# Mixture of experts on one core: down product one block later, weights in three buffers by expert

## The reference

```python
p_group = softmax(h @ w_rg + b_rg);  pg, grp = top_k(p_group, 1)
le_g = (h @ w_re + b_re)[group grp];  we, ei = top_k(softmax(le_g), 2)
gates = pg * we / sum(we)                      # two experts of each token
for e in range(16):
    a = silu(h @ w_eg[e]) * (h @ w_eu[e])      # 1024 -> 256, twice
    out = out + gates[:, e] * (a @ w_ed[e])    # 256 -> 1024
```

## Time and profile before

| | us |
|---|---|
| three runs | 1703.21, 1734.66, 1704.06 |
| median of them | 1704.06 |
| span of the profiled execution, first to last instruction | 1733.6 |
| time of the profiled execution | not listed by itself; of the three runs only the highest, 1734.66, is as long as its span |
| blocks 2 to 31 of the experts' stage | 1280 to 1669 of the span |

### The profile page before, as it was taken

How to read it: one execution, slowest core, us unless ns; L and a number is a source line. 1 busy time by engine, 2 the same in 40 slices (tenths; PEclk the granted TensorE clock), 3 DMA queues, 4 the chain that set the end, 5 groups by cost and what they waited for, 6 DMA issues and landing times.

```text
span 1733.6 us, 15660 instructions
## 1 busy us (share of the span) xinstructions
PE 1518.5 (88%) x5392; PEld 867.8 (50%) x5392; DVE 626.5 (36%) x1253; ACT 378.9 (22%) x788; POOL 135.1 (8%) x202
## 2 busy tenths in 40 slices
PE   7899999996099998999999999999589999999940
PEld 2575433432055473886777775455444444444420
DVE  2204339999813269611111232324401111111119
ACT  4114210030124210132233352111011111111114
POOL 0100100000000202101000000000021111111131
PEclk9899989998599869565555699999589999999975
DMA  9102652100030002406000000111198999999945
GB/s 348 43 1 97 192 184 76 49 1 0 0 73 1 3 25 70 125 2 157 0 1 0 1 1 25 68 66 41 47 355 329 336 335 331 332 343 323 341 166 188
DMA packets 78230, 219.98 MB, mean 127 GB/s; under 512 B 26205, under 2 KB 40733, under 8 KB 62791
## 3 DMA queue, kind: packets, MB, share of 16 engines
q1 hardware_dynamic: 61436, 163.70, 27.2%
q0 software_dynamic: 16736, 55.51, 8.8%
HBM read 191.07 MB, written 28.11 MB: 126 GB/s over the span
## 4 chain that ended last, share of the span: by engine, by line
PE 71%; DVE 13%; issue 11%; ACT 3%; DMA 1%; SPq 1%; DVEq 0%; POOL 0%; ACTq 0%; POOLq 0%
PE psum L1269 13%; PE psum L1208 7%; PE psum L878 7%; PE psum L1286 7%; PE psum L1132 7%; PE psum L1176 5%; DVE marks L1738 4%; PE psum L836 4%; PE psum L1162 4%; PE psum L901 2%; PE psum L1082 2%; PE psum L1144 1%; DVE mem L1669 1%; PE psum L1227 1%; PE psum L1278 1%
## 5 line engine op out<-in xcount | busy, mean ns | idle before, releaser
L878 PE MATMUL psum<-mem 128*128 128x512 f32 (+5 forms) x576 | 179.5, 471 | 61.2 <-ACT mem L1368 55.5
L1269 PE MATMUL psum<-mem 128*128 128x512 f32 x512 | 228.0, 599 | 1.1 <-ACT mem L1579 1.1
L901 PE MATMUL psum<-mem 128*128 128x512 f32 (+1 forms) x480 | 165.7, 511 | 0.0
L878 PEld LDWEIGHTS psum<-mem 128*128 128x128 f32 (+1 forms) x576 | 95.8, 186 | 137.4 <-issue 75.0
L1269 PEld LDWEIGHTS psum<-mem 128*128 128x128 f32 x512 | 98.3, 192 | 125.3 <-issue 123.8
L1949 DVE CUSTOM_DVE_ANT_0 mem<-psum,mem 128x1024 f32<-128x1024 f32 (+3 forms) x64 | 48.4, 758 | 242.1 <-PE psum L1132 242.1
L1286 PE MATMUL psum<-mem 128*128 128x512 f32 x256 | 118.4, 605 | 15.2 <-ACT mem L1589 15.2
L1208 PE MATMUL psum<-mem 128*128 128x512 f32 (+1 forms) x288 | 127.3, 602 | 0.7 <-issue 0.7
L901 PEld LDWEIGHTS psum<-mem 128*128 128x128 f32 x480 | 86.5, 212 | 79.4 <-issue 79.4
L1132 PE MATMUL psum<-mem 64*128 64x512 f32 (+3 forms) x192 | 118.2, 739 | 0.0
L1738 DVE TENSOR_SCALAR_CACHE_REDUCE marks<-mem,top_try_low 128x384 uint16<-128x384 uint16 (+6 forms) x112 | 104.0, 993 | 0.6
(11 more groups left out here) (338 smaller groups left out, 1618.1 us busy)
## 6 DMA issues: line engine op xcount, KB each, us to landing
mem<-in_w_exp_gate SPq DMA_DIRECT2D x32, 1024.0 KB, 6.3
mem<-in_w_exp_up SPq DMA_DIRECT2D x32, 1024.0 KB, 8.4
mem<-in_w_exp_down SPq DMA_DIRECT2D x32, 1024.0 KB, 8.3
mem<-in_w_ada SPq DMA_DIRECT2D x24, 1024.0 KB, 5.7
y_of_slot<-mem POOLq DMA_DIRECT2D x32, 512.0 KB, 7.6
mem<-in_x_prompt SPq DMA_DIRECT2D x16, 512.0 KB, 5.0
mem<-in_w_in SPq DMA_DIRECT2D x3, 2048.0 KB, 7.7
h_rows<-mem POOLq DMA_DIRECT2D x8, 512.0 KB, 2.9
```

The source lines that it names most:

```text
L878: mm = pe.matmul(bank[0:rows(i), to:to + width], h_t[:, k, cols(i)], w[:, k, c0:c0 + width], start=(k == 0), stop=(k == KT - 1))
L901: mm = pe.matmul(bank[0:width, 0:n_t], w[:, k, c0:c0 + width], h_t[:, k, t0:t0 + n_t], start=(k == 0), stop=(k == KT - 1))
L1269: mm = pe.matmul(psum[:, 2 + u, :].rearrange("p (n f) -> p n f", n=2), x_slot_t[:, u, k, :], w_gu[u][:, :, k, :], start=(k == 0), stop=(k ...
```

## The change

1. **Down one block late.** PE's order for block j becomes `gate_up(j)`, `turn_x(j+1)`, `down(j-1)`, `turn_hid(j)`. ACT copies the turned x of the next block before the turned hidden rows; DVE copies y of block j-1 after the product of block j.
2. **Three weight buffers by expert.** Expert e always sits in buffer e mod 3. DVE works out for each block the buffer's offset (`w_at_i`) and whether its expert differs from the block before (`is_new_i`), seven instructions where one was. Each expert gets at least one block, so that the experts follow one another without a gap. SP reads three numbers per block and issues the three loads under the condition `is_new`; a load that is left out still counts on its semaphore. PE reads the offset of each block and addresses the weights through a register.
3. **First ones ahead of the routing.** The weights of expert 0 are loaded as soon as the normed rows are all written, before the experts are known.
4. All five loops over pairs of blocks become straight code on their engines.

The core of the diff:

```diff
-        "full_before": np.broadcast_to(P * np.arange(TILES)[None, :], (P, TILES)),
+        "full_before": np.broadcast_to((P * np.arange(TILES) - (np.arange(TILES) == 0))[None, :], (P, TILES)),
+        "slot_step": np.broadcast_to(W_SLOT * np.append(np.diff(np.arange(NE) % W_SLOTS), 0)[None, :], (P, NE)),
...
+        W_DOWN = 2 * KT * DE
+        gate_up_at = lambda off: mem[:, bass.ds(off, W_DOWN)].rearrange("p (n k f) -> p n k f", n=2, k=KT)
+        down_at = lambda off: mem[:, bass.ds(off + W_DOWN, 2 * D)].rearrange("p (m d) -> p m d", m=2)
+        E0 = W_SLOT * W_SLOTS
...
+            def load_gate_up(j, e, to, needed):
                 for n, name in enumerate(("w_exp_gate", "w_exp_up")):
...
+                    sp.dma_start(gate_up_at(to)[:, n], we[name][bass.ds(e, 1)].rearrange("e (p k) f -> (e p) k f", k=KT),
+                                 **needed).then_inc(s_ew[j % W_SLOTS], 16)
...
+            def load_down(j, e, to, needed):
+                sp.dma_start(down_at(to), we["w_exp_down"][bass.ds(e, 1)].rearrange("e (p c) d -> (e p) c d", c=2),
+                             **needed).then_inc(s_ed[j % W_SLOTS], 16)
...
             sp.wait_ge(s_h2_turned, TILES)
             sp.wait_ge(s_h2, TILES)
-            for j in range(2):
-                e = load_expert(j, j)
-                if j == 0:
-                    sp.wait_ge(s_xs[0], 16)
-                load_down(e, j)
-            with sp.Fori(1, BLOCKS // 2) as jj:
-                for half in range(2):
-                    sp.wait_ge(s_gate_up, 2 * jj + half - 1)
-                    e = load_expert(2 * jj + half, half)
-                    sp.wait_ge(s_down, 2 * jj + half - 1)
-                    load_down(e, half)
+            load_gate_up(0, 0, 0, {})
+            load_down(0, 0, 0, {})
+            sp.wait_ge(s_experts_known, 1)
+            for j in range(1, BLOCKS):
+                e = sp.value_load(expert_i[0:1, j:j + 1], min_val=0, max_val=NE - 1)
+                to = sp.value_load(w_at_i[0:1, j:j + 1], min_val=0, max_val=W_SLOT * (W_SLOTS - 1))
+                is_new = sp.value_load(is_new_i[0:1, j:j + 1], min_val=0, max_val=1)
+                if j >= W_SLOTS:
+                    sp.wait_ge(s_gate_up, j - W_SLOTS + 1)
+                load_gate_up(j, e, to, {"cond": is_new})
+                if j >= W_SLOTS:
+                    sp.wait_ge(s_down, j - W_SLOTS + 1)
+                load_down(j, e, to, {"cond": is_new})
 
...
+            def weights_of(j):
+                return pe.value_load(w_at_i[0:1, j:j + 1], min_val=0, max_val=W_SLOT * (W_SLOTS - 1)) if j else 0
+
+            def gate_up(j, w_at):
+
+                u, w_gu = j % 2, gate_up_at(w_at)
...
+                pe.wait_ge(s_ew[j % W_SLOTS], 32 * (j // W_SLOTS + 1))
+                if j >= 2:
...
                 t.then_inc(s_hid_turned, 1)
+
+            def down(j, w_at):
+
+                u, w_dn = j % 2, down_at(w_at)
                 pe.wait_ge(s_hid_t, j + 1)
...
+                pe.wait_ge(s_ed[j % W_SLOTS], 16 * (j // W_SLOTS + 1))
+                if j >= 1:
                     pe.wait_ge(s_y_rows, j)
...
             turn_x(0, 0, 0, first=True)
...
+            pe.wait_ge(s_experts_known, 1)
+            w_at = [0] * BLOCKS
+            for j in range(BLOCKS):
+                w_at[j] = weights_of(j)
+                gate_up(j, w_at[j])
+                if j + 1 < BLOCKS:
+                    turn_x(j + 1, (j + 1) % 2, (j + 1) // 2)
+                if j >= 1:
+                    down(j - 1, w_at[j - 1])
+                turn_hid(j)
+            down(BLOCKS - 1, w_at[BLOCKS - 1])
...
+            keep_x(0)
+            for j in range(BLOCKS):
+                u = j % 2
                 act.wait_ge(s_gate_up, j + 1)
...
                 act.activation(silu_g[:, u, :], psum[:, 2 + u, 0:DE], ACT.Silu).then_inc(s_silu_g, 1)
+                if j + 1 < BLOCKS:
+                    keep_x(j + 1)
                 act.wait_ge(s_hid_turned, j + 1)
...
                 act.activation(hid_t[:, u, :, :], psum[:, 4 + u, 0:2 * P].rearrange("p (m t) -> p m t", m=2), copy).then_inc(s_hid_t, 1)
-                if not last:
-                    keep_x(j + 1, 1 - u, first=(first and u == 0))
...
             step(dve.tensor_reduce(expert_f, ended, AX.X, ALU.add))
-            dve.tensor_scalar(expert_i[:, :], expert_f[0:1, :], float(NE - 1), None, ALU.min).then_inc(s_experts_known, 1)
-
-
-            def expert_block(j, u, occurrence, first):
+            step(dve.tensor_scalar(expert_f, expert_f, float(NE - 1), None, ALU.min))
+            own.did(dve.tensor_copy(expert_i[:, :], expert_f[0:1, :]))
+            own.did(dve.memset(is_new_i[:, 0:1], 0))
+            own.did(dve.tensor_tensor(is_new_i[:, 1:], expert_f[0:1, 1:], expert_f[0:1, 0:BLOCKS - 1], ALU.subtract))
+            step(dve.tensor_tensor(ended, ended, K("slot_step").unsqueeze(1).to_broadcast([P, BLOCKS, NE]), ALU.mult))
+            step(dve.tensor_reduce(w_at_f, ended, AX.X, ALU.add))
+            dve.tensor_copy(w_at_i[:, :], w_at_f[0:1, :]).then_inc(s_experts_known, 1)
...
+            def keep_y(j):
+
...
+                dve.wait_ge(s_down, j + 1)
...
+                dve.tensor_copy(y_rows[:, u, :].rearrange("p (c d) -> p c d", c=2), psum[:, 6:8, :]).then_inc(s_y_rows, 1)
...
+            for j in range(BLOCKS):
+                u = j % 2
                 dve.wait_ge(s_silu_g, j + 1)
...
                 dve.tensor_tensor(hid[:, u, :], psum[:, 2 + u, DE:2 * DE], silu_g[:, u, :], ALU.mult).then_inc(s_hid, 1)
-                dve.wait_ge(s_down, j + 1)
...
+                if j >= 1:
+                    keep_y(j - 1)
+            keep_y(BLOCKS - 1)
```

More of the change, by code:

```diff
@@ L48 @@
 HIGH_BITS, LOW_BITS = 15, 16
+W_SLOTS, W_SLOT = 3, 6144
 def rows(i):
@@ L1261, in turn_x, with turn_hid @@
                 t.then_inc(s_x_slot_turned, 1)
-            def expert_block(j, u, occurrence, first, last):
+            def weights_of(j):
+                return pe.value_load(w_at_i[0:1, j:j + 1], min_val=0, max_val=W_SLOT * (W_SLOTS - 1)) if j else 0
+            def gate_up(j, w_at):
+                u, w_gu = j % 2, gate_up_at(w_at)
                 pe.wait_ge(s_x_slot_t, j + 1)
-                pe.wait_ge(s_ew[u], 32 * (occurrence + 1))
-                if not first:
+                pe.wait_ge(s_ew[j % W_SLOTS], 32 * (j // W_SLOTS + 1))
+                if j >= 2:
                     pe.wait_ge(s_hid, j - 1)
                 for k in range(KT):
-                    mm = pe.matmul(psum[:, 2 + u, :].rearrange("p (n f) -> p n f", n=2), x_slot_t[:, u, k, :], w_gu[u][:, :, k, :],
+                    mm = pe.matmul(psum[:, 2 + u, :].rearrange("p (n f) -> p n f", n=2), x_slot_t[:, u, k, :], w_gu[:, :, k, :],
                                    start=(k == 0), stop=(k == KT - 1))
                 mm.then_inc(s_gate_up, 1)
-                if not last:
-                    turn_x(j + 1, 1 - u, occurrence + u)
+            def turn_hid(j):
+                u = j % 2
                 pe.wait_ge(s_hid, j + 1)
-                if not first:
+                if j >= 2:
                     pe.wait_ge(s_hid_t, j - 1)
@@ L1291, in _ @@
             turn_x(0, 0, 0, first=True)
[L1292 to L1297, removed]
-                expert_block(BLOCKS - 2 + u, u, BLOCKS // 2 - 1, False, u == 1)
+            pe.wait_ge(s_experts_known, 1)
[9 more added lines that the diff above has]
+            down(BLOCKS - 1, w_at[BLOCKS - 1])
         @block.scalar
@@ L1572, in _, with keep_x @@
             act.activation(ids_i[:, :], psum[:, 2, 0:BLOCKS], copy).then_inc(s_ids_known, 1)
-            def keep_x(j, u, first=False):
+            def keep_x(j):
                 act.wait_ge(s_x_slot_turned, j + 1)
-                if not first:
+                if j >= 2:
                     act.wait_ge(s_gate_up, j - 1)
-                act.activation(x_slot_t[:, u, :, :].rearrange("p (c k) t -> p c (k t)", c=2), psum[:, 0:2, :], copy).then_inc(s_x_slot_t, 1)
-            def expert_block(j, u, first, last):
+                act.activation(x_slot_t[:, j % 2, :, :].rearrange("p (c k) t -> p c (k t)", c=2), psum[:, 0:2, :], copy).then_inc(s_x_slot_t, 1)
+            keep_x(0)
+            for j in range(BLOCKS):
+                u = j % 2
                 act.wait_ge(s_gate_up, j + 1)
-                if not first:
+                if j >= 2:
                     act.wait_ge(s_hid, j - 1)
                 act.activation(silu_g[:, u, :], psum[:, 2 + u, 0:DE], ACT.Silu).then_inc(s_silu_g, 1)
+                if j + 1 < BLOCKS:
+                    keep_x(j + 1)
                 act.wait_ge(s_hid_turned, j + 1)
-                if not first:
+                if j >= 2:
                     act.wait_ge(s_down, j - 1)
                 act.activation(hid_t[:, u, :, :], psum[:, 4 + u, 0:2 * P].rearrange("p (m t) -> p m t", m=2), copy).then_inc(s_hid_t, 1)
-                if not last:
-                    keep_x(j + 1, 1 - u, first=(first and u == 0))
```

(8 more changed lines are left out.)

37 lines of the change are left out of this document (12 added, 25 removed).

## The result

The changed kernel takes 1830.03 us in the median of 4 runs (1828.2 to 1831.65), the kernel before 1703.9; the ratio is 1.0745, 95% interval 1.0728 to 1.0762. The forecast was 1755, with a range of 1688 to 1805.

The account below looks back on a forecast made before the run. The prediction took PE to be bound by its own work and the handover inside a block; +27.6 (gather waits), +24 (clock), -1 (stage ends) and +1 (first loads) made +51 on 1704, so 1755 us, range 1688 to 1805.

Parts of the forecast that it names:

- the ring: Experts' stage: late down, store of y, next gather, x transposes, down again; period the larger of 12.0 and landing plus 7.3.
- blocks without a wait, and the stage's end: Experts' stage: 29 periods of 12.0 us instead of 12.56, and -1 for the ends of the stage; -17 us.
- clock behind the waits: PE's clock at half speed after waits: 1.7 us lost in each of the 6 and half of the 16 gathers; +24 us.
- first gather beside 3 MB: Stage start: expert 1's load can run beside the first gather, landing it 0 to 3.7 us later; +1 us taken.
- halfway, 6.2, for the 16: The 16 gathers that meet one load (1 or 2 MB) land in 6.2 us; 13.5 us a block.
- 8.0 for the 6: The 6 gathers that meet both loads (3 MB) land in 8.0 us, the earlier median; 15.3 us a block.
- L = 5.3 for the 16: Lower end of the forecast's own range: 16 gathers land in 5.3 us with a steady clock; +7 to +10 us.
- the gather in time: Rival: gathers still land in 4.3 to 4.7 us, all 29 periods take 12.0; 1687 us, chance 0.17.
- PE's register reads: Rival: PE's reads of weight offsets show, 0.77 to 3.9 us a block less 0.60; middle 1757 us, chance 0.06.
- The condition holds the loads back: Its rival: loads not held back, 4 MB a block move as before, every gather lands in 8.0; 1833 us, chance 0.05.
- The "wrong" mark of 330 GB/s: Sign against the forecast: DMAs in the experts' stage still moving 330 GB/s as before, instead of some 205.
- the sum carries over: Outside the experts' stage: the profiled execution's 29.5 us above the median lies elsewhere, so +51 applies to 1704 unchanged.

Follow-up runs that it names:

- e6: Changed kernel with POOL's gather issued ahead of the store of y, and the loads of blocks 1 and 2 behind the first gathers; 1701.76 us, once 1663.39.
- e3: Changed kernel with the down product back in its own block (PE, ACT and DVE in the old order), weights as changed; 1741.59 us.

## Why the prediction was wrong

The direction and the place were right: the ring through store, gather and `turn_x`. Its sizes, in us, over the stage:

| term | forecast | measured | from |
|---|---|---|---|
| blocks without a wait, and the stage's end | -17 | -34.2 | first `turn_x` to end: 373.7 in e6, 407.9 before |
| PE's waits for the gathers | +43.8 | +88.5 | the table above |
| PE running out at a wait | 0 | +4.2 | what is left, 0.2 a wait |
| clock behind the waits | +24 | +29.7 | 14 x 2.12 |
| first gather beside 3 MB | +1 | +4.6 | issue to `turn_x` 9.03, 4.42 before |
| **stage** | **+51** | **+92.8** | |
| ahead of the stage | 0 | +34.2 | first gather 1258.60, 1224.44 |

**The step that failed most is "halfway, 6.2, for the 16".** It put a load of 1 MB and one of 2 MB into one class between two landings of before. For down it fits (6.4). Gate and up are issued within half a microsecond of the gather, and it landed after 9.5. "8.0 for the 6" failed too (10.3): the 8.0 of before is from a steady stream, in which the gather goes out 2.6 us behind a down load and, in the same trace, 5.1 ahead of the next gate and up (1299.92). With the two measured waits in place of the two assumed, the sum is 1755 + 8 x 3.4 + 6 x 2.4 = 1797. That this meets the 1796 left when the stretch ahead is taken out (below) is partly luck: the other misses in the stage, -17 for the blocks and some +17 for the last three terms and the down loads, cancel. That 14 waits lost clock, as forecast, is luck too: the 8 of the 16 that did were those that waited 4.9 us, not 1.5. The range took 9.6 for the 6 as the worst, so the slowest landing of before was no bound. Its lower end was added up wrongly besides: L = 5.3 for the 16 gives 84 + 16 x 12.6 + 91.8 - 364.2 = +13, not +7 to +10.

**Blocks without a wait** took 11.42 us, not 12.0. I took PE's busy time for its own work. But each of the two waits of before also let PE run empty, which its rows book as busy. The two hidden transposes of before, then a block without a wait after the change:

```profile
1300.20 0.51 PE L1278 MATMUL psum<-const,mem 128*128 128x128 f32 x2 [0.22 <-DVE mem L2074]
```

```profile
1686.32 1.05 PE L1267 MATMUL psum<-const,mem 128*128 128x128 f32 x8
1687.21 3.60 PE L1304 MATMUL psum<-mem 128*128 x8
1690.64 0.39 PE L1292 MATMUL psum<-const,mem 128*128 128x128 f32 x2
1690.87 7.03 PE L1281 MATMUL psum<-mem 128*128 x16
1697.74 1.05 PE L1267 MATMUL psum<-const,mem 128*128 128x128 f32 x8
```

Without a wait the next row starts before the one ahead of it ends: `turn_x` takes 0.89 us of the block instead of 1.05, the hidden transposes 0.23 instead of 0.51, `down` 3.43 instead of 3.54 (1301.18 to 1304.72). That is 0.55, and with the 0.60 us of idle time it makes up the 1.14.

**The first loads ahead of the routing** came with a loss: with expert 0 loaded early, SP had the 3 MB of the next expert to issue, and nothing to hold them back, just as the first gather went out:

```profile
1258.43 0.35 SPq L655 DMA_DIRECT2D mem<-in_w_exp_gate  x1
1258.60 1.03 POOL L797 DMA_INDIRECT mem<-h_rows,ids_i  x1 [43.92 <-ACT ids_i L1594]
1258.97 0.35 SPq L655 DMA_DIRECT2D mem<-in_w_exp_up  x1
1259.52 0.34 SPq L659 DMA_DIRECT2D mem<-in_w_exp_down  x1
...
1267.63 1.95 PE L1267 MATMUL psum<-const,mem 128*128 128x128 f32 x8 [9.54 <-DMA mem<-h_rows,ids_i]
```

I had bounded that by 3.7 and taken 1; e6, which keeps the early loads and holds back the next ones, gives it back.

**Of the rivals**, the gather in time is out in 22 of 29 blocks. PE's register reads cost nothing: no idle time before `gate_up` in the stage at full pace, and 11.42 us a block. The condition holds the loads back: 169.85 MB moved, 219.98 before. The "wrong" mark of 330 GB/s did not appear; the 205 forecast were 180, since the stage was longer.

**The 34 us ahead of the stage** had no place in the sum. I saw that the one profiled execution was 29.5 over the median, and that the excess lay outside the stage, and treated it as a constant. That step, "the sum carries over", is the second that failed: it was a second outcome that the changed kernel took in all 4 launches. Without it the time would have been some 1796, inside the range and still 41 above the forecast.

## What to carry to other kernels

When a product is moved one step later, move what it feeds on the in-order queues too: here the gather issued ahead of the store on POOL turns +92.8 us in the stage into -34.3 (with the loads of blocks 1 and 2 held back), while the median of the launches stays at that of before. The Trainium skill, "Perfetto Trace Analysis", section on DMA optimizations, suggests separate issuing engines for inputs and outputs; that would cut this ring too, which no run here shows. A landing time belongs to what is issued beside it: price it by the bytes that start in the same microseconds, and do not carry one over from a steady stream.

## What was not expected

Halving the weights (330 to 224 GB/s at the same pace, in e3) changed nothing, but with the late gather the same bytes were worth 133 us. And the same instructions at the same busy share ran 140 or 218 us at half clock ahead of the stage, 32 us in the total, with odds that differ between kernels whose instructions differ only behind it.
